# Decoder block with a sparse expert layer: the preparation of further expert blocks is moved into the branch on their number, the last result is taken in two halves, and the first gathered rows are turned ahead of the first low parts

## What is computed

```python
def moe_ffn(h, router_w, router_b, w_gate_up, b_gate_up, w_down, b_down):
    ...
    top_logit, top_idx = lax.top_k(logits, TOP_K)
    gate = jax.nn.softmax(top_logit, axis=-1)
    ...
    def expert_block(args):
        x_blk, e = args
        gu = x_blk @ w_gate_up[e] + b_gate_up[e]
        g = jnp.minimum(gu[:, :D_FF], SWIGLU_LIMIT)
        u = jnp.clip(gu[:, D_FF:], -SWIGLU_LIMIT, SWIGLU_LIMIT)
        act = (u + 1.0) * (g * jax.nn.sigmoid(SWIGLU_ALPHA * g))
        return act @ w_down[e] + b_down[e]
    ...
    out = jnp.zeros((N, D), h.dtype).at[buf_token].add(yb * buf_gate[:, None].astype(yb.dtype))
```

## Time and profile before

| | |
|---|---|
| median of three runs | 2186.32 us |
| the profiled execution's own time | 2186.8 us |
| its span (first to last instruction) | 2185.2 us |
| TensorE busy | 2095.8 us (96%) |
| weight load busy | 1618.2 us (74%) |
| DVE busy | 1609.1 us (74%) |
| ACT busy | 1323.1 us (61%) |
| POOL busy | 850.5 us (39%) |
| mean granted TensorE clock | 0.985 |
| memory traffic | 515.19 MB, mean 236 GB/s |

### The profile page before, as it was taken

One profiled execution on the slowest core, in us unless ns is written; L12 is line 12 of the kernel. 1 busy time (PEld: TensorE's weight loads), 2 busy tenths in 40 slices (PEclk: granted clock), 3 DMA queues, 4 the chain that ended last, 5 costly groups with the idle time before them and its releaser, 6 DMA issues.

```text
span 2185.2 us, 38817 instructions
## 1 busy us (share of the span) xinstructions
PE 2095.8 (96%) x13480; PEld 1618.2 (74%) x13481; DVE 1609.1 (74%) x1604; ACT 1323.1 (61%) x1463; POOL 850.5 (39%) x698
## 2 busy tenths in 40 slices
PE   7989999999999997999999999999999999999995
PEld 7867777777777775777777777777887777777774
DVE  4165767676666466897897897898998778777885
ACT  4266675756444224676676676676876566665664
POOL 1120101010066344465665653454645334433376
PEclk9999999999999997999999999999999999999997
DMA  4101212122255538899999998999999899888992
GB/s 154 31 29 46 70 36 71 29 63 62 78 174 195 190 128 299 310 345 331 336 355 340 332 353 314 346 363 350 396 362 366 280 337 333 309 282 304 345 318 69
DMA packets 270040, 515.19 MB, mean 236 GB/s; under 512 B 37733, under 2 KB 80176, under 8 KB 269964
## 3 DMA queue, kind: packets, MB, share of 16 engines
q1 hardware_dynamic: 242308, 469.61, 59.7%
q0 software_dynamic: 20000, 39.16, 7.3%
q10 hardware_dynamic: 7656, 5.44, 0.8%
HBM read 475.83 MB, written 42.45 MB: 237 GB/s over the span
## 4 chain that ended last, share of the span: by engine, by line
PE 55%; POOL 3%; DVE 1%; issue 1%; DMA 1%; ACT 0%; POOLq 0%; DVEq 0%; ACTq 0%
PE ex_gu L2446 30%; PE ex_yp L2490 15%; PE ex_rest L2468 6%; PE ex_rest L2507 3%; POOL ex_xg L2141 1%; POOL ex_nxt_q L2136 1%; DVE ex_wlo L2298 1%; PE ex_tr L2406 1%; PE ex_gu L2406 1%; DMA out_dram<-ex_ytok,ex_piece 1%; PE ex_gu L2433 0%; DMA ex_nxt_q<-slots 0%; POOL out_dram L2148 0%; PE ex_yp L2437 0%; POOL ex_idx L2171 0%
## 5 line engine op out<-in xcount | busy, mean ns | idle before, releaser
L2298 DVE TENSOR_TENSOR ex_wlo<-ex_raw,ex_whi 128x2048 fp32r<-128x2048 f32 x387 | 872.9, 2286 | 138.6 <-ACT ex_whi L2031 132.5
L2031 ACT ACTIVATE ex_whi<-ex_raw 128x2048 fp32r<-128x2048 f32 x387 | 731.5, 1913 | 133.7 <-PE ex_gu L2446 115.0
L2141 POOL DMA_INDIRECT ex_xg<-xn_s,ex_idx x165 | 338.5, 2052 | 400.6 <-DVE ex_xrest L2348 346.8
L2446 PE MATMUL ex_gu<-ex_whi,ex_xhi 128*128 128x512 f32 x1024 | 284.9, 400 | 13.3 <-DVE ex_xlo L2357 13.1
L2446 PE MATMUL ex_gu<-ex_whi,ex_xlo 128*128 128x512 f32 x1024 | 275.5, 391 | 0.0
L2446 PE MATMUL ex_gu<-ex_wlo,ex_xhi 128*128 128x512 f32 x1024 | 274.5, 390 | 0.0
L2446 PEld LDWEIGHTS ex_gu<-ex_whi,ex_xhi 128*128 128x128 f32 x1024 | 186.4, 189 | 69.2 <-issue 21.6
L2446 PEld LDWEIGHTS ex_gu<-ex_whi,ex_xlo 128*128 128x128 f32 x1024 | 192.9, 188 | 41.6
L2446 PEld LDWEIGHTS ex_gu<-ex_wlo,ex_xhi 128*128 128x128 f32 x1024 | 192.6, 188 | 41.1
L742 POOL TENSOR_TENSOR at_wlo<-at_raw,at_whi 128x1024 fp32r<-128x1024 f32 x15 | 36.1, 2404 | 451.4 <-ACT at_whi L555 451.4
L58 PE MATMUL at_job<-xnT_hi,at_whi 128*128 128x512 f32 x416 | 178.6, 429 | 5.2 <-DVE at_nxt_qa L778 2.9
(11 more groups left out here) (379 smaller groups left out, 3494.6 us busy)
## 6 DMA issues: line engine op xcount, KB each, us to landing
ex_raw<-in_w_gate_up_dram SPq DMA_DIRECT2D x512, 512.0 KB, 8.3
ex_raw<-in_w_down_dram SPq DMA_DIRECT2D x256, 512.0 KB, 8.0
at_raw<-in_w_in_dram SPq DMA_DIRECT2D x25, 512.0 KB
gT<-at_gst SPq DMA_DIRECT2D x32, 256.0 KB, 2.3
mg_g<-gT SPq DMA_DIRECT2D x32, 256.0 KB, 3.9
raw_o<-in_w_out_dram SPq DMA_DIRECT2D x8, 512.0 KB, 5.6
op_x<-in_x_dram SPq DMA_DIRECT2D x8, 512.0 KB, 4.1
out_dram<-op_h SPq DMA_DIRECT2D x8, 512.0 KB, 2.8
```

Of the source, the lines that this page charges most:

```text
L2031: nc.scalar.activation(w_hi[:, i % RING, :], raw[:, i % SLABS, :], ACT.Copy).then_inc(hi_d, 1)
L2141: pool.indirect_dma_start(out=xg[:, a, :], out_offset=None, in_=xn_s.rearrange("t (q c) -> (t q) c", q=Q), in_offset=bass.IndirectOffsetOn ...
L2298: nc.vector.tensor_tensor(w_lo[:, slot, :], raw[:, i % SLABS, :], w_hi[:, slot, :].bitcast(F32), ALU.subtract).then_inc(lo_d, 1)
L2446: mm = nc.tensor.matmul(gu[:, half, h, :], x[:, k, :], w[:, kk, h, :], start=half == 0 and k == 0 and n == 0, stop=k == KD - 1 and n == 2)
```

## The change

`further_blocks` gets a function `begin`, called inside the branch on `nov`. What each engine did for the blocks 32 and 33 ahead of that branch moves into it (`begin_further` on ACT, POOL and DVE). For this, block 31 gets a body of its own on DVE, and `next_rows` is parted into `advance` and `next_rows`. `add_rows` now adds the rest first and then the full tile, in every block. `take_y_half` on ACT and on DVE replaces the last `take_y`. At the start DVE no longer waits for `ini`, and turns the rows ahead of the first splits.

```diff
--- before.py
+++ after.py
@@ -1955,11 +1955,13 @@
...
-        def further_blocks(eng, body):
+        def further_blocks(eng, body, begin=None):
...
             with eng.If(nov > 0):
+                if begin is not None:
+                    begin()
                 with eng.Fori(0, MAXOVER) as i:
@@ -2071,6 +2073,12 @@
...
+            def take_y_half(b):
+                act.wait_ge(slab_mm, SLABS * b + SLABS + RING)
+                act.wait_ge(cur_d, b + 1)
+                nc.scalar.activation(ytok[:, 0:HALF], yp[:, 0, :], ACT.Copy, scale=cur[:, 0, 1:2].bitcast(F32)).then_inc(y_ev, 1)
             def take_y_rest(b):
@@ -2083,7 +2091,7 @@
...
-            def body(b, last, first=False):
+            def body(b, over, first=False, last=False):
                 split_hi(b, AHEAD)
@@ -2099,23 +2107,32 @@
...
                 hidden_hi(b, 1)
-                take_x(b + 1)
+                if not last:
+                    take_x(b + 1)
                 hidden_rest(b)
-                for i in range(12, SLABS + AHEAD):
-                    split_hi(b, i)
                 if not last:
+                    for i in range(12, SLABS + AHEAD):
+                        split_hi(b, i)
+                if not last and not over:
                     act.wait_ge(raw_mm, SLABS * b + 10)
...
                 take_y_rest(b)
+            def begin_further():
+                take_x(NE)
+                for i in range(12, SLABS + AHEAD):
+                    split_hi(NE - 1, i)
             body(0, False, first=True)
...
                 body(b, False)
-            body(NE - 1, True)
-            nov = further_blocks(act, body)
-            take_y(nov + (NE - 1))
+            body(NE - 1, False, last=True)
+            nov = further_blocks(act, body, begin_further)
+            take_y_half(nov + (NE - 1))
@@ -2141,24 +2158,27 @@
...
-            def add_rows(b):
-                hold(pool, y_ev, b + 2, spare)
+            def add_rows(b, parts=1):
                 hold(pool, y2_ev, b + 2, spare)
-                pool.indirect_dma_start(out=out[0, :, :], out_offset=bass.IndirectOffsetOnAxis(
-                    ap=cur[:, 0, 0:1].bitcast(U32), axis=0), in_=ytok[:, :], in_offset=None,
-                    bounds_check=T - 1, oob_is_err=False, compute_op=ALU.add).then_inc(y_out, 16)
                 pool.indirect_dma_start(out=out.rearrange("a t (q c) -> (a t q) c", q=Q),
...
                                         bounds_check=T * Q - 1, oob_is_err=False, compute_op=ALU.add).then_inc(y_out, 16)
-            def next_rows(b, on_chip=True):
+                hold(pool, y_ev, b + 1 + parts, spare)
+                pool.indirect_dma_start(out=out[0, :, :], out_offset=bass.IndirectOffsetOnAxis(
+                    ap=cur[:, 0, 0:1].bitcast(U32), axis=0), in_=ytok[:, :], in_offset=None,
+                    bounds_check=T - 1, oob_is_err=False, compute_op=ALU.add).then_inc(y_out, 16)
+            def advance(b):
...
                 hold(pool, idx_d, 3 * b - 2, spare)
+            def next_rows(b, on_chip=True, late=0):
                 if on_chip:
@@ -2170,7 +2190,7 @@
...
                                             ALU.mult, ALU.add).then_inc(idx_d, 1)
-                hold(pool, idx_d, 3 * b - 1, spare)
+                hold(pool, idx_d, 3 * b - 1 + late, spare)
                 hold(pool, x_tr, 3 * b, spare)
@@ -2199,6 +2219,7 @@
...
             pool.wait_ge(ones_d, 4 + Q)
+            advance(1)
             next_rows(1)
@@ -2213,18 +2234,31 @@
...
                     scatter(t)
+                near_end = isinstance(b, int) and b >= NE - 2
+                if near_end and b == NE - 1:
+                    hold(pool, idx_d, 3 * b + 2, spare)
+                    return
                 hold(pool, idx_d, 3 * b + 3, spare)
-                if isinstance(b, int) and b == NE - 2:
-                    pool.wait_ge(tok_out, 16 * NT * TOPK)
-                next_rows(b + 2, on_chip=not over and (not isinstance(b, int) or b + 2 < NE))
+                advance(b + 2)
+                if not near_end:
+                    next_rows(b + 2, on_chip=not over)
+            def begin_further():
+                pool.wait_ge(tok_out, 16 * NT * TOPK)
+                next_rows(NE, on_chip=False, late=1)
+                advance(NE + 1)
+                next_rows(NE + 1, on_chip=False)
             for b in range(2 + NT):
...
             body(NE - 1, False)
-            nov = further_blocks(pool, body)
-            add_rows(nov + (NE - 1))
+            nov = further_blocks(pool, body, begin_further)
+            add_rows(nov + (NE - 1), parts=2)
+            pool.wait_ge(tok_out, 16 * NT * TOPK)
@@ -2357,19 +2391,19 @@
...
-            dve.wait_ge(ini, 1)
-            split_lo(0, 0)
             for a in range(Q):
...
             take_x(0)
+            for i in range(2):
+                split_lo(0, i)
             dve.wait_ge(*landed[Q - 1])
             turn_x_rest(0)
-            for i in range(1, AHEAD):
+            for i in range(2, AHEAD):
                 split_lo(0, i)
-            def body(b, over):
+            def body(b, over, last=False):
                 for i in range(AHEAD, 7):
@@ -2381,18 +2415,40 @@
...
                 hidden_lo(b, 1)
-                turn_x(b + 1, 0)
-                turn_x(b + 1, 1)
-                turn_x_rest(b + 1)
+                if not last:
+                    turn_x(b + 1, 0)
+                    turn_x(b + 1, 1)
+                    turn_x_rest(b + 1)
                 split_lo(b, 11)
-                take_x(b + 1)
+                if not last:
+                    take_x(b + 1)
+                    for i in range(12, SLABS + AHEAD):
+                        split_lo(b, i)
+            def begin_further():
+                turn_x(NE, 0)
+                turn_x(NE, 1)
+                turn_x_rest(NE)
+                take_x(NE)
                 for i in range(12, SLABS + AHEAD):
-                    split_lo(b, i)
+                    split_lo(NE - 1, i)
+            def take_y_half(b):
+                dve.wait_ge(slab_mm, SLABS * b + SLABS + RING)
+                dve.wait_ge(cur_d, b + 1)
+                nc.vector.tensor_scalar(ytok[:, HALF:D], yp[:, 1, :], cur[:, 0, 1:2].bitcast(F32), None, ALU.mult).then_inc(y_ev, 1)
             body(0, False)
...
             destinations()
-            over_blocks(dve, body, first=2)
+            with dve.Fori(2, NE - 1) as b:
+                body(b, False)
+            body(NE - 1, False, last=True)
+            nov = further_blocks(dve, body, begin_further)
+            take_y_half(nov + (NE - 1))
...
```

## The result

The changed kernel takes 2168.97 us (median of four runs, 2165.57 to 2169.83) against 2185.65 (2183.55 to 2188.81): a ratio of 0.992, with a 95% interval of 0.9902 to 0.9937. Run again five times, it gave 2169.12 us and 0.9919 (0.9905 to 0.9932). The sign was right. The size was not: I had forecast 11.8 us, and about 17 came, at the edge of the range: the range ended at 2168.5 us, the median of 2168.97 is just inside it, and the ratio of 0.992 (2168.2 of the 2185.65 us) just outside.

The account below looks back on a forecast made before the run. TensorE was taken to bound the expert stage, so only its start and the tail could gain: 9.0 + 2.8 = 11.8 us off 2186.3 gave 2174.5 us, with a range of 2168.5 to 2179.5 us.

Parts of the forecast that it names:

- TensorE's pace: Expert stage, 838 to 2161 us: TensorE busy 1320.7 of 1323 us, so work taken off other engines inside gives nothing.
- Part 2, the start: Before the first expert matmul: turning rows as pieces land starts TensorE earlier, a gain of 2.8 us.
- the 2.04 us behind it: At the start: the time from the last turn's end on DVE to TensorE's start, kept at 2.04 us.
- The 0.3 us for turns beside the gathers: At the start: turns on DVE slow the fourth gather by 0.3 us, read from a gather beside a memset.
- What is moved behind: First slabs' low parts, made after the rows' turns, are still ready in time, save a possible wait of some 0.4 us.
- Part 1 up to the landing: Tail: without preparation for blocks that do not exist, the last add lands at 2169.2 instead of 2178.2, 9.0 us earlier.
- 10.6 by the issue's end: Tail: the gain if the drain ends 9.4 us after the last issue's end, instead of 6.7 after the last landing.
- Rival 3: Tail: the long drain cleans up behind ten gathers and fifty loads; gain up to 15.6 + 2.8, 2168 us; chance 0.12.
- Rival 1: Tail: the drain has its own fixed length; the tail gains 6.8, in all 9.6, 2176.7 us; chance 0.12.
- Rival 2: Start: early turns hold up the gathers or a piece lands late; no gain there, 2177.3 us; chance 0.10.
- Rivals 4 and 5: 4: preparation runs anyway, 2183.5 us, chance 0.02. 5: DVE stalls fetching block 31's code, slower, 25 us give 2193, chance 0.02.
- Part 3 and the halves: Rest's add first in the loop: nothing. Halving the last copy: nothing in itself; without the rest's add as cover, 0.5 us.

Follow-up runs that it names:

- the kernel with the preparation on POOL: The changed kernel with POOL alone preparing blocks 32 and 33 ahead of the branch, nothing on DVE and ACT; its span ended at 2180.9 us.
- the preparation alone: The changed kernel with old start, one whole copy of the full result on ACT and full tile added first; ratio 0.9931 to the kernel before.
- the start alone: The kernel before with only the new start (no wait for `ini`, turns ahead of the first splits); ratio 0.9985 to the kernel before.

## Why the prediction was right in part and wrong in its size

- **TensorE's pace.** Right. The stage took 1322.6 to 1323.3 us in every kernel run, with other orders of the adds and with or without the three splits.
- **Part 2, the start: 2.8 forecast, 3.0 measured**, and 0.9985 by itself. The sum of landing, one turn and the 2.04 us behind it held. The 0.3 us for turns beside the gathers was not needed: the fourth gather took 0.95 us. Nor was it rightly read from the rows: the gather beside the memset was also the first of its five, and in the kernel with the preparation on POOL the first of five took 1.10 us (at 2161.22) with nothing on DVE. Of its 0.3 us at most some 0.14 are left for the memset. So the rule of the Trainium skill that I had weighed against the change ("SBUF — State Buffer", the box on DVE blocking SWDGE DMA, the DMAs that POOL issues) does not bite for these turns. For the splits it has its sign again: an add of 1.57 us took 3.09 beside them.
- **What is moved behind.** Right: TensorE got no new wait. The second slab's third pass was at 836.82, and its low part, from the piece of 4.49 us that began at 830.46, was ready at 834.95. One thing I had not named: ACT now waits for weights in block 0, 3.03 us before 840.21, 0.93 before 843.05 and 1.45 before 846.90. These are the splits of the slabs 5 to 7, and their loads did not move with TensorE: SP issues them from 833.49 on, 12.24 us behind the first gather, and in the kernel before it was 12.22 (837.47). The split of slab 5 ends at 842.13, and TensorE reaches that slab, behind the rest's matmuls, only at 850.60, so the waits are covered.
- **Part 1 up to the landing: 9.0 forecast, 9.0 measured.** The adds start 0.2 us earlier than reckoned (0.74 and 2.62 us after the last matmul, against 0.94 and 2.84) and land in 6.1 us instead of 5.9. The fixed 2.0 us and bytes over 436 GB/s of the Trainium skill ("DMA: Bandwidth & Descriptors", Anatomy of one DMA, SWDGE path) would be an estimated 3.2 us for the full tile, 2.9 less than the 6.1 measured; for an add into memory no run here comes near it.
- **The step that failed** is the one behind the landing: "Counted from the last landing it takes 6.7 us more ... I take the landing, 9.0". I carried the drain's distance over unchanged. Measured, it fell from 7.0 to 2.0 us, which is the 5 us missing from the forecast. I had both other values in the text, 10.6 by the issue's end and 15.6 by a drain that ends with the landing, and the measured 14.0 lies between them, nearer to the second. The error was to treat a distance as a constant when its cause was not in the trace. The preparation was the only large thing that stood ahead of it, and it was the thing removed: with it alone removed the distance is 2.0 us (the preparation alone), and with it left in place 6.8 (the start alone).
- **Rival 3** named the cause, with a chance of 0.12: cleaning up behind the preparation. Its 2168 us is the number nearest to the 2168.97 measured, and the range, which I said took in most of this rival, ended at 2168.5, above it. The runs show half of the rival. Small loads lengthen the distance (3.1 us with 25, 4.4 with 50), gathers hardly (2.2 to 2.3), and the whole preparation on POOL brings back 9.67 us from the last issue, with no splits on DVE or ACT. Gathers, which I had named beside the loads, cost their issue and, five of them, 0.2 to 0.3 us of drain.
- **Rival 1**, a drain of a fixed 16.07 us, is ruled out: POOL's drain lasts 7.5 to 17.9 us in these kernels. **Rival 2** is ruled out by the start alone. **Rivals 4 and 5** did not occur: 384 splits, and TensorE's longest wait behind its first is 0.9 us.
- **Part 3 and the halves.** "Worth nothing in itself" held: undoing halves and order together moved the tail by 0.03 us. That the rest's add first "matters, since that add fits into the time of the copies" was wrong: with the halves, the full add first ended 0.2 us earlier, since its landing takes 5.7 us and the rest's 4.6.

**What stays open.** Why small loads and the whole preparation lengthen the drain was not seen: in the kernel before, between the last landing at 2178.2 and the end, the busy share of the DMA engines is 0.00, and of the five engines none is busy. Ten gathers, or the index computations, were not run by themselves. Of the two forms offered (one distance from the landing, or the later of two), the run with 25 loads and the rest last fits neither.

## What to carry to other kernels

Preparation for a case that may not occur belongs behind the branch that decides on it, above all on the queue that also carries the last output: here it held the last landing back by 9 us, and another 5 us came in the drain of that queue. When a tail is costed, count what the queue's drain adds behind the last landing as a term of its own, and give it a range down to the least that any kernel shows, as long as its cause is unknown. Starting work as each piece lands, in place of behind an unrelated wait and another piece of work, was worth its full 3 us, because the stage from there to the last matmul runs at TensorE's pace (1322.6 to 1323.3 us in every kernel).

## What the hardware showed that I had not expected

- POOL's drain lasted 16.07 us with the preparation ahead of it and 8.5 without, and behind the last landing 6.8 and 1.7 of these, with a DMA busy share of 0.00 in both.
- The time to the first gather, in code that no experiment touched, went from 819.7 to 826.2 us from one kernel's execution to another's: 6.5 us, more than the start of the change is worth. A later first gather goes with a lower granted clock in short stretches ahead of it. In the kernel before (stretch, us, the engines' busy times and counts, granted clock, DMA share, GB/s):

```profile
100.00:200.00 100.00, 92.49 (x524) 70.55 (x523) 58.45 (x51) 61.80 (x89) 16.75 (x13) 0.98 0.10 30
700.00:760.00 60.00, 56.83 (x285) 45.50 (x283) 28.56 (x57) 15.84 (x22) 21.36 (x52) 0.97 0.60 201
```

  and in the changed kernel:

```profile
100.00:200.00 100.00, 92.47 (x532) 70.55 (x531) 57.95 (x51) 62.91 (x91) 16.78 (x13) 1.00 0.11 31
700.00:760.00 60.00, 56.83 (x307) 45.45 (x306) 28.97 (x67) 16.74 (x25) 22.43 (x55) 1.00 0.58 193
```

  TensorE's granted clock falls in a stretch in one execution and not in the other, in code that is the same in both. Of the eight stretches of 100 us up to 800 us, one is under 1.00 in each of the three executions with the earliest first gather (819.7 to 821.3), and three or four are in each of the six with the latest (824.1 to 826.2). That this makes the whole difference was not shown. In the two executions of the changed kernel the distances from the first gather to the first matmul, and from the last matmul to the landing and to the end, repeated to 0.1 us, and the stage between to 0.6, where whole times needed many runs to tell 0.2%.
- The rest's add, from a block of at most 128 tokens whose rest is empty, took as long to issue (1.57 us) as the full tile's (1.56), and landed after 4.3 to 4.6 us against 5.7 to 6.3.
